# Units of steps 18 and 20 placed between the K tiles of the step's dense block, in a two-layer decoder trunk on one core

## The chip, the cores and the metric

The kernel runs on 1 core of one Trainium2 chip. The metric is device time in microseconds of one execution, and a profile of one execution goes with it. All times below are from the profile or the timed runs.

## The reference

The reference is one inference step of a decoder trunk of 2 layers, width 1024, on 256 prompt tokens and 8 single-token samples (264 columns together). In each layer the input is projected once, three groups of mixer heads work side by side on the parts, their outputs are projected together, and an MLP follows:

```python
proj = jnp.einsum('btd,de->bte', x, w_in)
hq, hf, hi, hg, rq, rk, rv, rg, su = jnp.split(proj, cuts, axis=-1)
...
o_hg, s_hg_new = _chunked_gated_linear(silu(hq), k_hg, hi, log_f, s_hg)     # 6 heads, gated
...
o_rt, s_rt_new = _chunked_gated_linear(q_r, k_r, rv, log_f_r, s_rt)         # 6 heads, retention
...
y5, s_re_new, s_im_new = _s5_scan(su, ...)
y5 = jax.nn.gelu(y5)
y5 = y5 * jax.nn.sigmoid(y5 @ s5_glu_w + s5_glu_b)
mixed = jnp.concatenate([o_hg, o_rt, y5], axis=-1).astype(x.dtype) @ w_out
x = _layer_norm(ALPHA * x + mixed, ln1_w, ln1_b)
ff = jnp.square(jax.nn.relu(x @ w_up)) @ w_down
x = _layer_norm(ALPHA * x + ff, ln2_w, ln2_b)
```

The outputs are the new activations and the new states of the three head groups, for prompt and samples.

## The kernel before

Every engine has a program of its own, written out by hand, and the programs meet on semaphores. The large matrices are cut into blocks of 128 output rows and 1024 inputs (512 KB). One block is one **step**. A layer has steps 0 to 22 for the input projection (one tile of 128 features each: the state-space input, the gated heads, the retention heads, and in steps 17 to 22 six tiles of output gates), 23 to 30 for the output projection, and the steps of the MLP behind them.

In a step TensorE (PE) runs the **dense** block: eight K tiles, each 128 inputs deep, which add up into one of three stream banks of PSUM (`dense`, L1051). A block is either read as it lies, one float32 matmul for each K tile (L1084, "unsplit"), or split into a high and a low part first, three matmuls for each K tile (L1109, L1110, L1111). ScalarE (ACT) makes the high part (`split_high`, L1165, its instruction L1172), VectorE (DVE) the low part (L1642). The split parts have three slots. `UNSPLIT` (L188) says which steps stay unsplit: in layer 0 steps 18 to 22 are split, in layer 1 steps 19 to 22. When the last matmul of a dense block is done, the semaphore `chunk_done` rises. ACT and DVE read the stream bank only behind that.

Beside the dense blocks stand the **units**: small pieces of matmul work of the mixers, each writing one of four mix banks in turn (`MIX_BANKS`). A unit waits until the unit four places ahead of it has been copied out of the bank. The table `PLAN` (L91 and the `_plan` calls) gives each step a list of units, and PE's loop runs them behind the step's dense block, unless `STOPS` (L172) has numbers for the step. Then the first units of the list stand between K tiles, each behind the number of K tiles that is given:

```python
stops = STOPS[l].get(c, ())
for at, to, u in zip((0,) + stops, stops, PLAN[l][c]):
    dense(l, c, range(at, to))
    units[u[0]](l, u)
...
    dense(l, c, range(stops[-1] if stops else 0, 8))
...
for u in PLAN[l][c][len(stops):]:
    units[u[0]](l, u)
```

The units that matter here are these. Step 18 of layer 0: two `glu` units (L943, four long matmuls in all), then transposes on PE (`transposes`, all at L734): `tr_hkd` twice, `tr_rv_sample`, `tr_rk_sample`, `tr_rv` twice, then two `ret_score` (L907, L910). Step 18 of layer 1 has the same without `glu` and `tr_hkd`. Step 20 of both layers: `ret_kv` twice (L857), `ret_o` three times (L932 to L936), `ret_state` (L921).

ACT and DVE run in the order of their own programs, step by step, too. At its step 19 in layer 0 ACT first splits block 21 (L1172), which takes the slot of block 18 and so waits for `chunk_done` of step 18, then does the gate sigmoid of step 18's tile (`gate_sigmoid`, L1222), then the sigmoid of the two `glu` banks (L1316), the copies of the two `tr_hkd` banks (L1326), of `tr_rv_sample` (L1349), of `tr_rk_sample` (L1352) and of `tr_rv` (L1356). In layer 1 the split of block 21 comes a step later there, because its load waits for the unsplit block 18. At its step 21 DVE first does the output gate of step 20's tile (`output_gate`, L1941, behind ACT's sigmoid of that tile), then adds the two `ret_kv` banks to the retention state and so empties them (`ret_sample_add`, L1966). `ret_k_decay` (L1983) on DVE empties the banks of two transposes of step 17.

The queue of SyncE (SP) loads the weight blocks in order into three raw slots, each behind the last reader of the block that lay there. GpSimd (POOL) prepares the masked inputs of `ret_kv`.

Of the kernel before, what the change touches and what calls it, by code (L numbers as in the profile page):

```python
# [43 lines left out]
UP_A = OUT0 + KT  # L44
# [49 lines left out]
def _plan(step, *names, layers=range(DEPTH)):  # L94
    for layer in layers:
        PLAN[layer][step] += names
# [72 lines left out]
for _l in range(DEPTH - 1):  # L169
    _plan(TABLES_AT, *[("s5_tab_in", _l + 1, _t) for _t in range(4)], layers=(_l,))  # L170
    _plan(N_CHUNKS - 1, ("s5_tab_near", _l + 1), layers=(_l,))
STOPS = ({19: (3, 6), 21: (4,), 22: (2, 5, 6, 7), UP_A + 1: (3, 5)}, {17: (3, 6), 21: (4,), 22: (2, 4, 6), UP_A + 1: (3, 5)})  # L172
UNITS_OF = {"s5_out": lambda u: [], 
            **{_n: lambda u: [u[:1]] if u[1] == 0 else [] for _n in ("hg_o_sample", "ret_o_sample")},
            **{_n + "_shift": lambda u: [u[:1]] if u[1] == 0 else [] for _n in ("ln1", "ln2")},
# [36 lines left out]
def build(nc, xT, weights, vectors, matrices, constants, level_masks, state_hg, state_rt, state_s5,  # L212
          y_out, hg_p_out, rt_p_out, s5_p_out, hg_s_out, rt_s_out, s5_s_out):
    with ExitStack() as ctx:
# [422 lines left out]
        def _(pe):  # L637
# [481 lines left out]
            for l in range(DEPTH):  # L1119
                for c in range(N_CHUNKS):  # L1120
# [10 lines left out]
                    if c == UP_A:  # L1131
# [6 lines left out]
                        continue  # L1138
                    stops = STOPS[l].get(c, ())
                    for at, to, u in zip((0,) + stops, stops, PLAN[l][c]):  # L1140
# [1342 lines left out]
```

How the kernel before makes its waits and increments, by code:

```python
        def wait_unit(eng, l, name):  # L470
            if name[0] == "hg_level":
                r, h = name[1:]
                eng.wait_ge(level_done[h], 7 * l + r + 1)
            elif name[0] == "hg_far":
                eng.wait_ge(far_done[name[1]], l + 1)
            elif name[0] == "ret_score":
                eng.wait_ge(score_done[name[1] % 2], 3 * l + name[1] // 2 + 1)
            else:
                eng.wait_ge(unit_done, UNITS_DONE[l, name])
# [7 lines left out]
        def need(eng, s, n):  # L488
            if n > 0:
                eng.wait_ge(s, n)
# [13 lines left out]
        def wait_raw(eng, n):  # L505
            eng.wait_ge(raw_loaded[RAW_SLOT[n]], 16 * RAW_TURN[n])
# [1 line left out]
        def wait_raw_read(eng, n):  # L509
            if SPLIT[n]:
                eng.wait_ge(low_ready, split_count(n))
            else:
                eng.wait_ge(chunk_done, n + 1)
# [1 line left out]
        def dense_tile(eng, l, c):  # L516
            eng.wait_ge(chunk_done, l * N_CHUNKS + c + 1)
            g = l * N_TILES + tile_index(c)
            return stream_bank[g % STREAM_BANKS][:, 0:T], tile_free[g % STREAM_BANKS]
# [4 lines left out]
        @block.sync  # L525
# [5 lines left out]
            for n in range(1, DEPTH * N_CHUNKS):  # L531
                if n in (1, 2):
                    sp.wait_ge(x_loaded[2 * n - 1], 16)
                if RAW_PREV[n] is not None:
# [3 lines left out]
                sp.wait_ge(y_ready, m + 2)  # L538
                sp.dma_start(y_out[:, m:m + 2, :], X[:, m:m + 2, :]).then_inc(outs["y"], 16)
            sp.wait_ge(outs["y"], 16 * KT // 2)
```

## Time and profile before

| | |
|---|---|
| median of 3 runs | 746.35 us (746.32 to 747.8) |
| the profiled execution, its own time | 746.15 us |
| its span, first to last instruction | 744.3 us, 17116 instructions |
| PE busy | 709.1 us (95%) |
| PE weight loads busy | 652.6 us (88%) |
| DVE busy | 539.3 us (72%) |
| ACT busy | 403.2 us (54%) |
| mean granted clock of PE | 0.982 of 2.4 GHz |

Times in the views count from the start of the span. Layer 0's steps 18 to 20 lie between 112 and 138 us, layer 1's between 482 and 501 us. A float32 matmul shows as two records, so a count of x8 at L943 is four matmuls. The busy time of a matmul includes its way through the array, so the pace of a run of matmuls is read from the starts, not from the durations.

### The profile page before, as it was taken

Reading aid. Unit: us, or ns where it says so; the run is one execution under the profiler, and the core shown is the slowest. Engines: PE = TensorE matmul, PEld = TensorE weight load, DVE = VectorE, ACT = ScalarE, POOL = GpSimd, SP = SyncE. Lnnn points to the kernel's source line nnn. Section 1 sums busy time; section 2 is a strip of 40 time slices with the busy share of each in tenths; the row PEclk is TensorE's granted clock in tenths of the full one; section 3 lists DMA queues with packets and bytes.
Section 4 is the critical chain, followed back from the end, with each engine's and each line's share of the span. In section 5 each row is a group of like instructions: output and inputs, shape, how many; then the busy total and the mean of one; then the engine's idle time right before and its main releaser. Section 6 shows DMA issues by size and latency. Waiting matters only on the chain.

```text
span 744.3 us, 17116 instructions
## 1 busy us (share of the span) xinstructions
PE 709.1 (95%) x7028; PEld 652.6 (88%) x7028; DVE 539.3 (72%) x970; ACT 403.2 (54%) x761; POOL 43.4 (6%) x62
## 2 busy tenths in 40 slices
PE   8899799999999999999979899999999999999994
PEld 6787668778999999999969797877999999999993
DVE  7999775468788988965685886556878776555474
ACT  4521055446788467764558233355568755677342
POOL 3000012100000000000040001020000000000001
PEclk9999899999999999999989999999999999999998
DMA  8733134535565656555624312342646656666631
GB/s 287 277 115 88 41 97 152 190 116 168 148 194 168 195 175 188 182 170 170 177 67 138 110 38 86 133 163 55 216 119 200 187 176 179 190 174 188 177 114 59
DMA packets 31085, 112.88 MB, mean 152 GB/s; under 512 B 3648, under 2 KB 3888, under 8 KB 30624
## 3 DMA queue, kind: packets, MB, share of 16 engines
q1 hardware_dynamic: 28224, 100.78, 44.3%
q0 software_dynamic: 2208, 9.93, 3.6%
q8 instruction: 56, 0.92, 0.5%
q10 hardware_dynamic: 576, 1.08, 0.4%
q14 instruction: 21, 0.17, 0.1%
HBM read 107.20 MB, written 4.18 MB: 150 GB/s over the span
## 4 chain that ended last, share of the span: by engine, by line
PE 78%; DVE 7%; ACT 3%; issue 2%; DVEq 0%; ACTq 0%
PE stream L1109 21%; PE stream L1110 20%; PE stream L1111 20%; PE stream L1084 6%; PE mix L812 1%; DVE w_low L1642 1%; PE mix L1007 1%; PE mix L845 1%; PE mix L885 1%; PE mix L734 1%; PE mix L857 0%; DVE scratch L1989 0%; PE mix L994 0%; DVE scratch L2237 0%; PE y_bank L715 0%
## 5 line engine op out<-in xcount | busy, mean ns | idle before, releaser
L1642 DVE TENSOR_TENSOR w_low<-w_raw,w_high 128x1024 fp32r<-128x1024 f32 x161 | 196.9, 1224 | 106.9 <-ACT w_high L1172 105.5
L1172 ACT ACTIVATE w_high<-w_raw 128x1024 fp32r<-128x1024 f32 x161 | 170.4, 1058 | 152.2 <-PE stream L1111 138.9
L1109 PE MATMUL stream<-a_high,w_high 128*128 128x264 f32 x520 | 154.9, 298 | 5.3 <-DVE a_low L2251 5.3
L1110 PE MATMUL stream<-a_low,w_high 128*128 128x264 f32 x520 | 148.7, 286 | 0.0
L1111 PE MATMUL stream<-a_high,w_low 128*128 128x264 f32 x520 | 148.4, 285 | 0.0
L1109 PE MATMUL stream<-h_high,w_high 128*128 128x264 f32 x512 | 146.3, 286 | 0.0
L1111 PE MATMUL stream<-h_high,w_low 128*128 128x264 f32 x512 | 145.1, 283 | 0.0
L1110 PE MATMUL stream<-h_low,w_high 128*128 128x264 f32 x512 | 145.0, 283 | 0.0
L1109 PEld LDWEIGHTS stream<-a_high,w_high 128*128 128x128 f32 x520 | 99.1, 191 | 9.7 <-issue 8.0
L1110 PEld LDWEIGHTS stream<-a_low,w_high 128*128 128x128 f32 x520 | 99.5, 191 | 0.4
L1111 PEld LDWEIGHTS stream<-a_high,w_low 128*128 128x128 f32 x520 | 98.9, 190 | 0.0
L1084 PE MATMUL stream<-X,w_raw 128*128 128x264 f32 x400 | 95.5, 393 | 3.2 <-DMA w_raw<-in_weights 2.5
L1109 PEld LDWEIGHTS stream<-h_high,w_high 128*128 128x128 f32 x512 | 96.4, 188 | 0.5 <-DVE h_low L2222 0.4
L1110 PEld LDWEIGHTS stream<-h_low,w_high 128*128 128x128 f32 x512 | 96.5, 188 | 0.1
L1111 PEld LDWEIGHTS stream<-h_high,w_low 128*128 128x128 f32 x512 | 96.0, 188 | 0.0
L1084 PEld LDWEIGHTS stream<-X,w_raw 128*128 128x128 f32 x400 | 74.6, 191 | 21.0 <-issue 6.2
L1109 PE MATMUL stream<-pre_a,w_high 128*128 128x266 f32 x256 | 74.6, 291 | 0.0
L1111 PE MATMUL stream<-pre_a,w_low 128*128 128x266 f32 x256 | 72.9, 285 | 0.0
L1110 PE MATMUL stream<-pre_x,w_high 128*128 128x266 f32 x192 | 54.8, 286 | 0.0
L1109 PEld LDWEIGHTS stream<-pre_a,w_high 128*128 128x128 f32 x256 | 48.3, 189 | 2.7 <-issue 2.6
L1111 PEld LDWEIGHTS stream<-pre_a,w_low 128*128 128x128 f32 x256 | 48.2, 188 | 0.0
L1110 PEld LDWEIGHTS stream<-pre_x,w_high 128*128 128x128 f32 x192 | 36.4, 189 | 0.1
(393 smaller groups left out, 983.1 us busy)
## 6 DMA issues: line engine op xcount, KB each, us to landing
w_raw<-in_weights SPq DMA_DIRECT2D x189, 512.0 KB, 3.6
mats<-in_matrices POOLq DMA_DIRECT2D x2, 1024.0 KB, 6.6
S_hg<-in_state_hg POOLq DMA_DIRECT2D x2, 768.0 KB, 7.4
out_hg_s<-S_hg POOLq DMA_DIRECT2D x2, 768.0 KB, 4.1
consts<-in_constants POOLq DMA_DIRECT2D x1, 1499.5 KB, 8.5
X<-in_xT ACTq DMA_DIRECT2D x4, 264.0 KB, 5.0
out_y<-X SPq DMA_DIRECT2D x4, 264.0 KB, 2.1
S_rt<-in_state_rt POOLq DMA_DIRECT2D x2, 512.0 KB, 8.5
```

The source lines that it names most:

```text
L734: mm = pe.transpose(b[0:rows, 128 * i:128 * i + 128], src[:, i, cols], ident)
L812: mm = pe.matmul(banks[h][to:to + n, n * (2 * f + t):n * (2 * f + t) + n], kd[rows, f, left], qd[rows, f, right], start=True, stop=True, t ...
L845: mm = pe.matmul(b[64 * h:64 * h + 64, :].rearrange("p (b v) -> p b v", b=8), ks_tok[:, 128 * ft + 64 * h:128 * ft + 64 * h + 64], v_own[V ...
L885: mm = pe.matmul(b[:, at:at + 2], qs_hg[:, ft, 2 * bp:2 * bp + 2, :].rearrange("p b v -> p (b v)"), cv("pair_sum")[:, 0:2], start=True, st ...
L1007: mm = pe.matmul(b[at:at + BLOCK, 0:T], cv("model_mean")[:, 0:BLOCK], src[:, k, :], start=(k < first + 4), stop=(k >= KT - 4), tile_positi ...
L1084: mm = pe.matmul(bnk[:, 0:T], w_raw[:, RAW_SLOT[n], 128 * k:128 * k + 128], x[:, k, :], start=(kk == 0), stop=(kk == 7))
L1109: pe.matmul(bnk[:, 0:width], wh, xh, start=(first and kk == 0), stop=False)
L1110: pe.matmul(bnk[:, 0:width], wh, xl, start=False, stop=False)
L1111: mm = pe.matmul(bnk[:, 0:width], wl, xh, start=False, stop=(last and kk == 7))
L1172: act.activation(w_high[:, SPLIT_SLOT[n], :], w_raw[:, RAW_SLOT[n], :], ACT.Copy).then_inc(high_ready, 1)
L1642: put(tt(w_low[:, SPLIT_SLOT[n], :], w_raw[:, RAW_SLOT[n], :], w_high[:, SPLIT_SLOT[n], :].bitcast(F32), ALU.subtract), low_ready)
```

## The change

The change adds entries for steps 18 and 20 to `STOPS` in both layers. In step 18 of layer 0 the first four units stand behind 2, 4, 6 and 7 K tiles, elsewhere the first three behind 2, 4 and 6. No instruction that computes is added or taken away, and the programs of ACT, DVE, POOL and SP stay as they are.

```diff
-STOPS = ({19: (3, 6), 21: (4,), 22: (2, 5, 6, 7), UP_A + 1: (3, 5)}, {17: (3, 6), 21: (4,), 22: (2, 4, 6), UP_A + 1: (3, 5)})
+STOPS = ({18: (2, 4, 6, 7), 20: (2, 4, 6), 19: (3, 6), 21: (4,), 22: (2, 5, 6, 7), UP_A + 1: (3, 5)}, {17: (3, 6), 18: (2, 4, 6), 20: (2, 4, 6), 21: (4,), 22: (2, 4, 6), UP_A + 1: (3, 5)})
```

**PE, layer 0, the end of step 18.** Here `stream0` is the dense block's bank and `mix0` to `mix3` are the mix banks. Before, from the last dense matmul on (the two `glu`, the two `tr_hkd`, the sample transposes, the two `tr_rv`, the scores):

```order
L1111 MATMUL stream0<-a_high,w_low 128x264
L943 MATMUL mix3<-MIX,mats 128x264 x2
L943 MATMUL mix0<-MIX,mats 128x264 x2
L734 MATMUL mix1<-consts,scratch 128x128 x3
L734 MATMUL mix2<-consts,scratch 128x128 x3
L734 MATMUL mix3<-consts,MIX 8x128 x3
L734 MATMUL mix0<-consts,KR 8x128 x2
L734 MATMUL mix1<-consts,MIX 128x128 x3
L734 MATMUL mix2<-consts,MIX 128x128 x3
L907 MATMUL mix3<-QR,KR 128x256
L907 MATMUL mix0<-QR,KR 128x256
```

With the change, from the first `tr_hkd` on:

```order
L734 MATMUL mix1<-consts,scratch 128x128 x3
L1109 MATMUL stream0<-a_high,w_high 128x264
L1110 MATMUL stream0<-a_low,w_high 128x264
L1111 MATMUL stream0<-a_high,w_low 128x264
L734 MATMUL mix2<-consts,scratch 128x128 x3
L1109 MATMUL stream0<-a_high,w_high 128x264
L1110 MATMUL stream0<-a_low,w_high 128x264
L1111 MATMUL stream0<-a_high,w_low 128x264
L734 MATMUL mix3<-consts,MIX 8x128 x3
L734 MATMUL mix0<-consts,KR 8x128 x2
L734 MATMUL mix1<-consts,MIX 128x128 x3
L734 MATMUL mix2<-consts,MIX 128x128 x3
```

Four units have moved ahead of the last K tile (the two `glu` stand behind two and four K tiles, above this piece), and the units behind the dense block begin with the one that writes `mix3` again, the bank of the first `glu`.

**ACT, layer 0, its step 19**, the same before and with the change; in brackets the semaphores that each instruction waits for:

```order
L1172 ACTIVATE w_high<-w_raw 128x1024 [waits chunk_done,raw_loaded0]
L1222 ACTIVATE late<-stream0 128x264 [waits chunk_done]
L1316 ACTIVATE X1<-mix3,vecs 128x264 [waits unit_done]
L1316 ACTIVATE X1<-mix0,vecs 128x264 [waits gel_ready,unit_done]
L1326 ACTIVATE scratch<-mix1 128x384 [waits gel_ready,unit_done]
L1326 ACTIVATE scratch<-mix2 128x384 [waits kt_ready,unit_done]
L1349 ACTIVATE late<-mix3 8x384 [waits kt_ready,unit_done]
L1352 ACTIVATE late<-mix0 8x256 [waits vs_ready,unit_done]
```

Nothing has moved here: the copies out of the mix banks stand behind two instructions that wait for a dense block.

**PE, layer 0, the end of step 20.** Before, behind the dense block (`ret_kv` twice, `ret_o` three times, `ret_state`):

```order
L857 MATMUL mix2<-late 32x512 x4
L857 MATMUL mix3<-scratch,late 32x512 x2
L932 MATMUL mix0<-scratch,V_tok 64x128 x2
L934 MATMUL mix0<-scratch,V_tok 64x128 x2
L936 MATMUL mix0<-scratch,V_tok 64x128 x2
L932 MATMUL mix1<-scratch,V_tok 64x128 x2
L934 MATMUL mix1<-scratch,V_tok 64x128 x2
L936 MATMUL mix1<-scratch,V_tok 64x128 x2
L932 MATMUL mix2<-scratch,V_tok 64x128 x2
L934 MATMUL mix2<-scratch,V_tok 64x128 x2
L936 MATMUL mix2<-scratch,V_tok 64x128 x2
L921 MATMUL mix3<-V_tok,scratch 32x64 x12
```

With the change, from the last K tile on:

```order
L1109 MATMUL stream2<-a_high,w_high 128x264
L1110 MATMUL stream2<-a_low,w_high 128x264
L1111 MATMUL stream2<-a_high,w_low 128x264
L932 MATMUL mix1<-scratch,V_tok 64x128 x2
L934 MATMUL mix1<-scratch,V_tok 64x128 x2
L936 MATMUL mix1<-scratch,V_tok 64x128 x2
L932 MATMUL mix2<-scratch,V_tok 64x128 x2
L934 MATMUL mix2<-scratch,V_tok 64x128 x2
L936 MATMUL mix2<-scratch,V_tok 64x128 x2
L921 MATMUL mix3<-V_tok,scratch 32x64 x12
```

Both `ret_kv` and the first `ret_o` have moved ahead of the last K tiles. The third `ret_o` and `ret_state`, which write the banks of the two `ret_kv` again, stay behind the dense block.

## Rows read from the trace of the kernel before

**Rows 1.** The page's chain that ended last, shares of the span.

```profile
PE 78%; DVE 7%; ACT 3%; issue 2%; DVEq 0%; ACTq 0%
```

**Rows 2.** Timeline of PE, step 18 of layer 0: start, length, instruction [idle before].

```profile
112.49 0.39 PE L1109 MATMUL stream<-a_high,w_high 128*128 128x264 f32 x1
112.71 0.29 PE L1110 MATMUL stream<-a_low,w_high 128*128 128x264 f32 x1
...
115.50 1.94 PE L943 MATMUL mix<-MIX,mats 128*128 128x264 f32 x8
117.28 0.82 PE L734 MATMUL mix<-consts,scratch 128*128 128x128 f32 x6
117.94 0.49 PE L734 MATMUL mix<-consts,MIX 128*8 128x128 f32 x3
...
120.61 0.70 PE L907 MATMUL mix<-QR,KR 32*128 32x256 f32 x4 [0.65 <-ACTq L1163]
...
121.47 0.39 PE L1109 MATMUL stream<-a_high,w_high 128*128 128x264 f32 x1
```

**Rows 3.** Timeline of ACT, the same stretch.

```profile
115.77 1.06 ACT L1172 ACTIVATE w_high<-w_raw 128x1024 fp32r<-128x1024 f32 x1 [2.90 <-PE stream L1111]
...
120.05 0.37 ACT L1352 ACTIVATE late<-mix 8x256 f32<-8x256 f32 x1
```

**Rows 4.** Timeline of DVE, the same stretch.

```profile
113.05 0.99 DVE L1983 TENSOR_TENSOR scratch<-mix,consts 128x256 f32<-128x256 f32 x2
```

**Rows 5.** Timeline of PE, step 20 of layer 0.

```profile
132.85 0.28 PE L1111 MATMUL stream<-a_high,w_low 128*128 128x264 f32 x1
...
133.95 1.02 PE L857 MATMUL mix<-scratch,late 8*32 8x512 f32 x4
134.90 0.44 PE L932 MATMUL mix<-scratch,V_tok 128*64 128x128 f32 x4
...
137.59 0.39 PE L1109 MATMUL stream<-a_high,w_high 128*128 128x264 f32 x1
```

**Rows 6.** Timeline of ACT and DVE, step 20 of layer 0.

```profile
133.18 0.39 ACT L1222 ACTIVATE late<-stream 128x264 f32<-128x264 f32 x1 [1.72 <-PE stream L1111]
...
134.24 1.63 DVE L1966 SCALAR_TENSOR_TENSOR S_rt<-S_rt,consts,mix 128x512 f32<-128x512 f32 x2
```

**Rows 7.** Timeline of ACT and PE, step 18 of layer 1.

```profile
486.64 0.39 ACT L1222 ACTIVATE late<-stream 128x264 f32<-128x264 f32 x1 [1.43 <-PE stream L1084]
...
488.14 0.70 PE L907 MATMUL mix<-QR,KR 32*128 32x256 f32 x4 [0.33 <-ACTq L1163]
```

**Rows 8.** Timeline of PE and DVE, step 20 of layer 1.

```profile
495.56 0.28 PE L1111 MATMUL stream<-a_high,w_low 128*128 128x264 f32 x1
...
498.05 1.63 DVE L1966 SCALAR_TENSOR_TENSOR S_rt<-S_rt,consts,mix 128x512 f32<-128x512 f32 x2
...
499.89 0.64 PE L921 MATMUL mix<-V_tok,scratch 128*32 128x64 f32 x24
...
500.46 0.39 PE L1109 MATMUL stream<-a_high,w_high 128*128 128x264 f32 x1
```

**Rows 9.** Stretches: length, busy time (records) of each engine, PE clock, DMA.

```profile
88.00:90.00 2.00, 0.00 (x0) 0.00 (x0) 0.00 (x0) 0.00 (x0) 0.00 (x0) 1.00 0.42 162
148.00:150.00 2.00, 1.13 (x10) 0.44 (x8) 1.68 (x4) 1.36 (x4) 0.00 (x0) 1.00 0.34 47
151.00:151.25 0.25, 0.25 (x3) 0.20 (x2) 0.20 (x1) 0.25 (x1) 0.00 (x0) 0.80 0.50 197
152.00:154.00 2.00, 2.00 (x9) 0.84 (x9) 1.58 (x3) 0.48 (x1) 0.00 (x0) 0.50 0.00 0
154.50:154.75 0.25, 0.25 (x2) 0.22 (x2) 0.25 (x1) 0.25 (x2) 0.00 (x0) 0.87 0.00 0
```

**Rows 10.** Timeline of PE, the same matmuls of step 23 and 24 in both layers.

```profile
153.25 4.01 PE L1084 MATMUL stream<-MIX,w_raw 128*128 128x264 f32 x14
...
512.24 3.38 PE L1084 MATMUL stream<-MIX,w_raw 128*128 128x264 f32 x14
```

## The prediction

> **What bounds the kernel now.** I read the chain that ended last first [rows 1]: 78% of the span lies on PE, 2% on issue and nothing on a DMA, so what delays PE in a stage delays the end unless a later wait takes it back. Then PE's timeline of step 18 in layer 0 [rows 2]: eight K tiles from 112.49 to 115.50, then the step's units, then step 19 at 121.47. The reader should see that this tail lasts 5.97 us and that PE waits in it, 0.65 us at the last pair of scores, for ACT. ACT's timeline says why [rows 3]: ACT idles 2.90 us until "PE stream L1111", the last dense matmul, and only then starts a row of work: the split of weight block 21 (its slot was step 18's, so it waits for that step's dense block), the gate sigmoid of step 18's tile, and behind them, in ACT's order, the copies that empty the four mix banks, down to L1352 at 120.05 (0.37 long). PE's L907 follows 0.19 later. So the tail is not a PE chain. It is an ACT chain of 121.47 - 115.50 = 5.97 us that begins where the dense block ends.
>
> **Step 18, layer 0.** The two glu units and two of the transposed units now stand in front of the last K tile, so the dense block ends later by what they take. Glu: 117.28 - 115.50 = 1.78 us for two. Transposes: 117.94 - 117.28 = 0.66 for six, 0.11 each [rows 2]. A dense run that starts behind a short unit is slow once: 112.71 - 112.49 = 0.22 to the second matmul, against (115.50 - 112.71)/23 = 0.12 for the other steps; 0.10 more, twice here (behind the long glu matmuls I take nothing): 0.20. One new wait: the first glu would stand at 112.49 + 0.22 + 5 x 0.12 = 113.31, and its bank is freed by DVE's first L1983 [rows 4], 113.05 + about 0.42 + about 0.19 until PE moves (estimates: a pair of 0.99 us with a gap in it, and the gap seen behind L1352) = 113.66: 0.35. Sum 1.78 + 0.66 + 0.20 + 0.35 = 3.0 us. ACT starts its chain 3.0 us later, and the chain is as long as before, since none of its copies waited for the units that move; the units left behind find their banks 3.0 later. PE, with less to do, idles some 2 us behind the dense block, and step 19 starts late by **3.0**. Bounds: 2.4 (units alone) and 3.3 (0.10 behind each glu too, and a little).
>
> **Step 20, layer 0.** Moved ahead of the last K tiles: both ret_kv and the first ret_o. Prices [rows 5]: the first ret_kv with the gap ahead of it 133.95 - (132.85 + 0.12) = 0.98, the second 134.90 - 133.95 = 0.95; the three ret_o and the state take 137.59 - 134.90 = 2.69, of which the state is 0.57 (500.46 - 499.89 in rows 8), so 0.71 for one ret_o. With three run starts of 0.10 the dense block ends 0.98 + 0.95 + 0.71 + 0.30 = 2.94 later. What hangs on that end [rows 6]: the gate sigmoid of step 20's tile, released by PE L1111; behind it DVE's output gate; behind that, in DVE's order, the two L1966 that empty the two ret_kv banks, the very banks that the third ret_o and the state need. L1966 starts 134.24 - 132.97 = 1.27 after the dense end. From there to the next step is 500.46 - 498.05 = 2.41 in layer 1, where the state did wait for the second L1966: 498.05 + 1.63 = 499.68, state at 499.89 [rows 8]. So the new tail is 1.27 + 2.41 = 3.68 us, however little PE has left. Before, it was 137.59 - 132.97 = 4.62, PE work that covered this chain; that cover goes. Net 2.94 + 3.68 - 4.62 = **2.0**; 1.6 with no run starts and no gap.
>
> **Step 18, layer 1.** Three transposed units, eight transposes at 0.11, move ahead: 0.88, and about 0.1 for run starts in all (the K tiles are single long matmuls here). ACT's gate sigmoid is released by PE L1084 and the copies of the first two banks stand behind it; PE already waits 0.33 for them at the scores [rows 7]. Net **1.0**, bounds 0.9 and 1.2. Weight block 21 is loaded when this dense block is done, so SP's queue moves by 1.0 too; the block is due at 500.46 [rows 8], over ten us on, and that costs nothing. POOL's blocks for ret_kv get their inputs later by the same shift, with as long to go.
>
> **Step 20, layer 1.** Same prices, 2.94, same tail, 3.68; before it was 500.46 - (495.56 + 0.12) = 4.78 [rows 8]. Net 2.94 + 3.68 - 4.78 = **1.8**; 1.4 at the least.
>
> Sum: 3.0 + 2.0 + 1.0 + 1.8 = **+7.8 us**, bounds 6.3 and 8.6. No PE wait further on takes it back: what PE waits for at the end of the mixer is DVE and ACT work that itself starts from PE units. The profiled execution took 746.15, 0.20 below the median of 746.35, so I add to the median: 754.2.
>
> **The clock.** PE's clock falls where its work thins out [rows 9]: in 148 to 150 PE worked 1.13 of 2 us, at 151.0 to 151.25 the granted clock is 0.80 on its way down, 152 to 154 lies at 0.50 (1.2 GHz), at 154.50 to 154.75 it is 0.87 on its way up: some 3.3 us at half rate, 1.65 us if PE has work throughout. A pair of rows agrees [rows 10]: fourteen L1084 records took 4.01 in layer 0, of which 154.5 - 153.25 = 1.25 us lay at the low clock, and 3.38 in layer 1: 0.63, half of 1.25. Not every gap does it: 88 to 90 stood still at full clock. The new tail of step 18 in layer 0 has 2.1 us of PE work in 6.0 (eleven transposes 1.21, scores 121.47 - 120.61 = 0.86), a longer thin stretch than 148 to 150, so I take one fall there: +1.65. By the Trainium skill, TensorE: Matmul & The Clock Gate, Part 1, the throttled clock is the default and activity lifts it; by that rule a tail this thin falls back to it and the time is 755.8, and without it 754.2. The trace agrees at 151 and not at 88. The other tails are shorter (3.7 us, half of it work); I take no fall there.
>
> 754.2 + 1.65 = **755.8 us**.
>
> **The rivals.** The waits as worked out, but no fall: 754.2, at the least 752.6. More falls, in the tails of step 20 too: 757.5, or 759.1 with two more.
>
> **Faster:** units between K tiles give ACT and DVE time to empty the banks, and PE's waits in the tails go. In layer 0's step 18 they are 5.97 less PE's work (1.78 + 0.66 + 1.21 + 0.86 = 4.51), 1.46; in layer 1's 0.33 [rows 7]; less run starts of 0.2 + 0.3 + 0.1 + 0.3 = 0.9: a gain of 0.9, 745.4. It decides from the point where ACT can empty a bank before the dense block has ended. Against it stands rows 3: ACT's first instruction there is released by the last dense matmul, and the copies stand behind it. The Trainium skill, Perfetto Trace Analysis, Matmuls, says that independent groups should rotate through different PSUM banks so that the evacuation of one overlaps the next group's matmuls; by that rule this change gains and the time is 745.4. The trace disagrees here: the banks rotate, but the evacuations stand behind a wait for the very block that they should overlap.
>
> **No change:** a later wait absorbs the delays, 746.4. For it speak PE's waits at the mixer's end; against it that they begin from PE's own units. That the change does not do what it says is excluded by the order of the built program.
>
> **How the numbers follow.** One fall 0.50, and its number is my time; no fall 0.22; more falls 0.18; faster 0.04; no change 0.04; 0.02 for a slowdown that I have not seen. The range 752.6 to 758.6 takes in the first two with their bounds and the nearer part of the third. Slower by over 0.2% (1.5 us, about what a measurement of this kernel can tell from no change) 0.92, within it 0.04, faster 0.04.
>
> **What would show it.** In the profile after, the dense block of step 18 in layer 0 takes 6.0 us from its first to its last matmul instead of 3.0, ACT's L1172 is still released by its end, and PE waits about 2 us for ACT at L734 behind it; in step 20 PE waits for DVE at L932 and L921, about 1.5 us together, in both layers; the clock lies at 0.50 for some 3 us in step 19 of layer 0. I am wrong if ACT's copies start before the dense end, if PE's new waits there stay under 1 us, or if step 21 of layer 0 starts 4 us late or more and the delay is gone by the up-projection.

## The result: slower by 15 us, where 9 were forecast

| | before | after |
|---|---|---|
| median | 746.34 us (745.1 to 747.8, 4 runs) | 761.73 us (761.39 to 764.23, 4 runs) |
| ratio to before, 95% interval | | 1.020 (1.017 to 1.023) |
| the profiled execution, and its span | 746.15 us, 744.3 us | 764.23 us, 762.3 us |
| mean granted clock of PE | 0.982 | 0.970 |

The direction was right and the size wrong: +15.4 us, and 761.7 lies above the range of 752.6 to 758.6. In the batches below the kernel before ran from 745.2 us (mean granted clock 0.983) to 752.4 us (0.973) from one execution to the next, so a part of a kernel is read from profiled executions stage by stage, and whole times only through ratios.

**Where it went.** Start of a step's first dense matmul in PE's timeline, less the same start in the profile of before (us; L0 is layer 0; each column is one of the kernels told of below):

| start of | before | after | a_18_l0 | b_20 | i_l1 | d_no19 | k_glu | e_act | f_act_dve | h_20_dve | j_best |
|---|---|---|---|---|---|---|---|---|---|---|---|
| L0 step 18 | 112.49 | 1.84 | -0.58 | -0.87 | 1.12 | 0.01 | -0.25 | -0.48 | 1.05 | -0.53 | 0.76 |
| L0 step 19 | 121.47 | 5.24 | 2.75 | -0.92 | 1.08 | 3.58 | 2.61 | -1.01 | 0.52 | -0.57 | 0.22 |
| L0 step 20 | 129.96 | 12.55 | 10.06 | -0.92 | 1.07 | 7.49 | 2.62 | -1.02 | 0.51 | -0.58 | 0.22 |
| L0 step 21 | 137.59 | 14.98 | 10.11 | 3.00 | 1.07 | 9.90 | 2.61 | 1.40 | 1.39 | 0.29 | 0.22 |
| L0 step 25 | 161.30 | 13.40 | 10.11 | 3.00 | 1.12 | 9.89 | 1.02 | -0.19 | 1.39 | -1.29 | -1.38 |
| L1 step 18 | 482.77 | 14.89 | 13.38 | 3.10 | 3.54 | 10.01 | 3.03 | 0.03 | 4.48 | 2.63 | 0.46 |
| L1 step 19 | 488.99 | 15.70 | 13.37 | 3.09 | 4.35 | 10.83 | 3.03 | -0.37 | 4.08 | 2.62 | 0.06 |
| L1 step 20 | 492.66 | 15.69 | 13.37 | 3.08 | 4.35 | 10.84 | 3.03 | -0.37 | 4.09 | 2.62 | 0.06 |
| L1 step 21 | 500.46 | 17.95 | 13.36 | 5.33 | 6.61 | 13.09 | 3.03 | 1.89 | 4.81 | 3.33 | 0.53 |

A difference between two lines of a column is what a stage added. In the changed kernel: step 18 of layer 0 3.40 (forecast 3.0), **step 19 7.31** (forecast 1.65, the clock), step 20 2.43 (2.0), step 18 of layer 1 0.81 (1.0), step 20 of layer 1 2.26 (1.8). The 1.84 ahead of step 18 is no part of the change: the program is the same up to there. It is most of the 2.5 us by which this profiled execution lies above the median.

PE's timeline of the changed kernel, step 18 of layer 0 and the starts of steps 19 and 20, answers to [rows 2] (start, length, instruction, idle before and its releaser):

```profile
114.32 0.39 PE L1109 MATMUL stream<-a_high,w_high 128*128 128x264 f32 x1
...
120.10 0.28 PE L1111 MATMUL stream<-a_high,w_low 128*128 128x264 f32 x1
122.39 0.49 PE L734 MATMUL mix<-consts,MIX 128*8 128x128 f32 x3 [2.00 <-ACTq L1163]
...
125.29 1.06 PE L907 MATMUL mix<-QR,KR 32*128 32x256 f32 x4 [0.63 <-ACTq L1163]
...
126.71 0.59 PE L1109 MATMUL stream<-a_high,w_high 128*128 128x264 f32 x1
127.09 0.42 PE L1110 MATMUL stream<-a_low,w_high 128*128 128x264 f32 x1
127.31 0.42 PE L1111 MATMUL stream<-a_high,w_low 128*128 128x264 f32 x1
...
142.51 0.40 PE L1109 MATMUL stream<-a_high,w_high 128*128 128x264 f32 x1
```

A dense block ends where its last L1111 starts, plus the 0.12 us from one of its matmuls to the next: here 120.10 + 0.12 = 120.22. The dense block now takes 120.22 - 114.32 = 5.90 us (6.0 was forecast), and PE then idles 2.00 us for ACT. In step 19 the matmuls start 0.22 apart where they started 0.12 apart in [rows 2]. ACT's timeline of the changed kernel, against [rows 3]:

```profile
120.49 1.06 ACT L1172 ACTIVATE w_high<-w_raw 128x1024 fp32r<-128x1024 f32 x1 [5.89 <-PE stream L1111]
...
124.73 0.37 ACT L1352 ACTIVATE late<-mix 8x256 f32<-8x256 f32 x1
```

ACT's chain still starts behind the last dense matmul and is as long as it was: L1352 ends 120.05 + 0.37 - 115.50 = 4.92 us after the dense end in [rows 2, 3], and 124.73 + 0.37 - 120.22 = 4.88 here. PE's waits in the changed kernel (us in total, times, longest), against 0.65 and 0.33 at L907 [rows 2, 7] and none at L932:

```profile
PE mix L932 <- DVEq L1621: 2.5, 2, 1.2
PE mix L734 <- ACTq L1163: 2.2, 2, 2.0
...
PE mix L907 <- ACTq L1163: 1.8, 2, 1.1
```

PE's timeline, step 20 of layer 0, against [rows 5]:

```profile
143.24 0.28 PE L1111 MATMUL stream<-a_high,w_low 128*128 128x264 f32 x1
143.45 1.06 PE L857 MATMUL mix<-late 8*32 8x512 f32 x8
144.44 0.39 PE L1109 MATMUL stream<-a_high,w_high 128*128 128x264 f32 x1
...
148.79 0.28 PE L1111 MATMUL stream<-a_high,w_low 128*128 128x264 f32 x1
...
151.12 0.44 PE L932 MATMUL mix<-scratch,V_tok 128*64 128x128 f32 x4 [1.24 <-DVEq L1621]
...
152.57 0.39 PE L1109 MATMUL stream<-a_high,w_high 128*128 128x264 f32 x1
```

And the stretches of the changed kernel (length, PE busy and records, granted clock, DMA share, GB/s), against [rows 9]:

```profile
120.00:122.00 2.00, 0.39 (x4) 1.00 0.73 219
122.00:124.00 2.00, 1.37 (x8) 1.00 0.29 70
124.00:126.00 2.00, 1.31 (x8) 0.88 0.65 236
126.00:128.00 2.00, 2.00 (x12) 0.50 0.03 8
...
140.00:142.00 2.00, 2.00 (x32) 0.50 0.48 182
142.00:144.00 2.00, 2.00 (x26) 0.86 0.00 0
...
162.00:164.00 2.00, 1.14 (x8) 1.00 0.53 213
```

PE works 3.07 of 6 us from 120 to 126; then the clock lies at 0.50 from 126 to 142, with PE's records filling every stretch. With the 0.48 us at half rate in 124 to 126 (0.12 x 2 / 0.5) and 0.56 in 142 to 144, that is some 17 us at 1.2 GHz. The fall of [rows 9] at 151 is gone: its place, now 162 to 164, shows 1.00, and 1.58 come back between steps 21 and 25.

### The profile page after: what moved, and what is told of

Read it like the earlier page. It is cut to its first block, busy times and chain, and to the rows that moved or that the text cites. A ratio compares the mean times of both kernels' runs of the same rounds, so it can differ in the third digit from the quotient of the medians.

```text
span 762.3 us, 17116 instructions
## 1 busy us (share of the span) xinstructions
PE 723.6 (95%) x7028; PEld 664.4 (87%) x7028; DVE 539.7 (71%) x970; ACT 403.2 (53%) x761; POOL 43.1 (6%) x62
## 3 DMA queue, kind: packets, MB, share of 16 engines
q10 hardware_dynamic: 576, 1.08, 0.4%
## 4 chain that ended last, share of the span: by engine, by line
PE 78%; DVE 7%; ACT 3%; issue 2%; DVEq 0%; ACTq 0%
PE stream L1109 21%; PE stream L1110 20%; PE stream L1111 20%; PE stream L1084 6%; PE mix L812 1%; DVE w_low L1642 1%; PE mix L885 1%; PE mix L734 1%; PE mix L1007 1%; PE mix L845 1%; PE mix L943 1%; PE mix L857 1%; DVE scratch L1959 0%; DVE scratch L1989 0%; PE mix L994 0%
## 5 line engine op out<-in xcount | busy, mean ns | idle before, releaser
L1109 PE MATMUL stream<-a_high,w_high 128*128 128x264 f32 x520 | 157.8, 304 | 5.3 <-DVE a_low L2251 5.3
L1110 PE MATMUL stream<-a_low,w_high 128*128 128x264 f32 x520 | 150.3, 289 | 0.0
L1111 PE MATMUL stream<-a_high,w_low 128*128 128x264 f32 x520 | 150.0, 288 | 0.0
L1111 PE MATMUL stream<-h_high,w_low 128*128 128x264 f32 x512 | 145.1, 283 | 0.0
L1109 PEld LDWEIGHTS stream<-a_high,w_high 128*128 128x128 f32 x520 | 100.7, 194 | 13.6 <-issue 11.9
L1110 PEld LDWEIGHTS stream<-a_low,w_high 128*128 128x128 f32 x520 | 101.2, 195 | 0.5
L1111 PEld LDWEIGHTS stream<-a_high,w_low 128*128 128x128 f32 x520 | 100.6, 193 | 0.0
L1084 PE MATMUL stream<-X,w_raw 128*128 128x264 f32 x400 | 99.6, 405 | 0.9 <-DMA X<-in_xT 0.6
L1111 PEld LDWEIGHTS stream<-h_high,w_low 128*128 128x128 f32 x512 | 96.0, 188 | 0.0
L1084 PEld LDWEIGHTS stream<-X,w_raw 128*128 128x128 f32 x400 | 77.7, 199 | 18.8 <-issue 3.9
L1111 PE MATMUL stream<-pre_a,w_low 128*128 128x266 f32 x256 | 72.9, 285 | 0.0
L1111 PEld LDWEIGHTS stream<-pre_a,w_low 128*128 128x128 f32 x256 | 48.2, 188 | 0.0
```

The source lines that it names most:

```text
L1084: mm = pe.matmul(bnk[:, 0:T], w_raw[:, RAW_SLOT[n], 128 * k:128 * k + 128], x[:, k, :], start=(kk == 0), stop=(kk == 7))
L1109: pe.matmul(bnk[:, 0:width], wh, xh, start=(first and kk == 0), stop=False)
L1110: pe.matmul(bnk[:, 0:width], wh, xl, start=False, stop=False)
L1111: mm = pe.matmul(bnk[:, 0:width], wl, xh, start=False, stop=(last and kk == 7))
```

## The experiments

The theories: **T1**, in step 18 ACT's chain hangs on the end of the dense block, so what stands ahead of that end is paid in full; **T2**, in step 20 DVE's two L1966, which empty the `ret_kv` banks, hang on the end of the dense block in the same way, through the output gate ahead of them; **T3**, the tail of layer 0's step 18 is so thin that the clock falls behind it. Rivals: the cut-up dense block itself costs the time (run starts), or the clock would fall there in any case. Where an expectation calls a rival T2 or T3, it means the rival that it states there.

### Parts alone: a_18_l0, b_20, i_l1

`a_18_l0` has the new stops of step 18 in layer 0 alone, `b_20` those of step 20 in both layers, `i_l1` those of steps 18 and 20 in layer 1.

```diff
-STOPS = ({19: (3, 6),
+STOPS = ({18: (2, 4, 6, 7), 19: (3, 6),
```

> Step 18 of layer 0 alone has its units between K tiles. Theory T1 (the tail behind the dense block is an ACT chain, and the thin tail drops PE's clock): step 19 starts 3.4 us late as in the changed kernel, the clock falls at the end of that tail and stays at 0.50 for 10 us or more, costing 5 us or more; with the old fall at 151 us gone, some 754 us. Rival T2 (the clock's falls are a matter of chance, only the waits belong to the change): 3.4 us over the kernel before, 749.8 us.

```diff
-STOPS = ({19: (3, 6),
+STOPS = ({20: (2, 4, 6), 19: (3, 6),
...
-{17: (3, 6),
+{20: (2, 4, 6), 17: (3, 6),
```

> Step 20 of both layers alone has its units between K tiles. T1: the dense block ends 2.9 us later and the DVE chain behind it stays, +2.0 and +1.8 us, no new fall of the clock: 750.2 us, PE waiting for DVE at L932 and L921. Rival T3 (thin units between K tiles by themselves lower the clock): a low clock in or behind step 20 of either layer, 753 us or more.

```diff
-{17: (3, 6),
+{18: (2, 4, 6), 20: (2, 4, 6), 17: (3, 6),
```

> The change in layer 1 alone, layer 0 as before. Theory (the waits as in the changed kernel's profile): step 18 adds 0.8, step 20 adds 2.3, sum 3.1 us, 749.5 beside 746.4, and no fall of the clock beyond those of the kernel before. Rival (the changed kernel's losses in layer 1 come from layer 0's delay): under 1 us. Second rival (falls of the clock also come behind layer 1's tails): 5 us or more.

Measured: `a_18_l0` 759.56 us (757.09 to 762.32), ratio 1.0146 (1.0097 to 1.0196). Its step 18 adds 3.33 and its step 19 7.31, to the hundredth what the changed kernel's step 19 added. The time is above the 754 expected: the fall cost more than 5 us, and the fall of [rows 9] did not go (0.50 in 162 to 164). `b_20` 753.96 (750.13 to 757.66), 1.0074 (1.0043 to 1.0105): 2.25 in layer 1 and 3.92 in layer 0, where a short fall lay inside step 20 (0.86, 0.50 and 0.79 in the three stretches from 132 to 138, 3.4 us at half rate). Its first two stretches:

```profile
132.00:134.00 2.00, 2.00 (x10) 0.86 0.00 0
134.00:136.00 2.00, 2.00 (x15) 0.50 0.00 0
```

So the low clock in step 20 came that the rival of `b_20` names; the time, 0.74% or 5.5 us above the kernel before, lies between the theory's 3.8 and the rival's 6.6 or more. PE's records fill these stretches and the one ahead of them, so no thin tail explains this fall; what does stays open. `i_l1` 752.64 (748.29 to 754.65), 1.0047 (1.0023 to 1.0071), some 3.5 us: 0.81 for step 18 and 2.26 for step 20, the changed kernel's increments, without layer 0's delay. So the parts add up within their intervals, and most of the loss, 1.5% of 2.0%, comes from one of the four places, layer 0's step 18.

### PE's gap filled: c_fill

The changed kernel with 16 dense matmuls of no use behind the dense block of layer 0's step 18, and four more ahead of the second pair of scores; they write the bank that step 19 then starts afresh.

```diff
 for u in PLAN[l][c][len(stops):]:
+    if l == 0 and c == 18 and u[0] == "tr_rv_sample":
+        fill(16)
+    if l == 0 and c == 18 and u == ("ret_score", 4):
+        fill(4)
     units[u[0]](l, u)
```

> The changed kernel with 16 dense matmuls more behind the dense block of step 18 in layer 0 and 4 more ahead of its last scores; they write a bank that step 19 clears, into time in which PE waits. T1: the waits stay, the clock does not fall at the tail, and the 7 us that step 19 lost at half rate come back: 754 to 755 us. T2 and T3: PE's wait is filled to no use, 761.7 us or a little more.

PE's timeline of this kernel (the filler is L1121), and its stretches:

```profile
110.88 0.39 PE L1109 MATMUL stream<-a_high,w_high 128*128 128x264 f32 x1
...
116.76 2.10 PE L1121 MATMUL stream<-a_high,w_high 128*128 128x264 f32 x16
...
122.68 0.39 PE L1109 MATMUL stream<-a_high,w_high 128*128 128x264 f32 x1
...
131.19 0.39 PE L1109 MATMUL stream<-a_high,w_high 128*128 128x264 f32 x1
```

```profile
122.00:124.00 2.00, 2.00 (x19) 1.00 0.06 25
124.00:126.00 2.00, 2.00 (x20) 1.00 0.20 83
...
134.00:136.00 2.00, 2.00 (x9) 0.73 0.00 0
```

Step 18 took 122.68 - 110.88 = 11.80 us, 2.82 more than before: twenty matmuls more cost nothing, because PE was waiting. Step 19 took 8.51 us instead of 8.49, at full clock. The time is 755.69 us (753.3 to 760.05), ratio 1.010 (1.0035 to 1.0165): 6.0 below the changed kernel, though PE does more. A fall of 3.4 us now lies inside step 20, between 134 and 140, as in `b_20`. This is T3 shown: with the gap filled, the long fall is not there. The mean clocks of the other executions fit: 0.981 to 0.985 in three of the four, against 0.969 to 0.976 in the changed kernel; the fourth, of 760.05 us, has 0.974. And 2.82 is T1's price at full clock.

### Step 19 left whole: d_no19

In the changed kernel step 19 of layer 0 is itself cut by units after three and six K tiles. Here it is not.

```diff
-STOPS = ({18: (2, 4, 6, 7), 20: (2, 4, 6), 19: (3, 6), 21: (4,),
+STOPS = ({18: (2, 4, 6, 7), 20: (2, 4, 6), 21: (4,),
```

> The changed kernel with the dense block of step 19 in layer 0 left whole (its three units stand behind it). T1 with the addition that a low clock lasts as long as PE's dense work is cut up by thin units: the fall is there, but full clock returns within or just behind step 19, about 4 us sooner than in the changed kernel: 758 to 760 us. Rival (the length of the low stretch does not depend on that): 761.7 us.

The stretches:

```profile
122.00:124.00 2.00, 1.31 (x8) 0.82 0.77 250
124.00:126.00 2.00, 2.00 (x12) 0.50 0.01 4
...
128.00:130.00 2.00, 2.00 (x11) 0.50 0.78 283
130.00:132.00 2.00, 2.00 (x20) 0.98 0.00 0
132.00:134.00 2.00, 2.00 (x24) 0.88 0.06 12
134.00:136.00 2.00, 2.00 (x24) 0.50 0.73 254
136.00:138.00 2.00, 2.00 (x34) 0.77 0.03 4
```

The fall comes at the same place but ends at 130, when step 19's unbroken dense block has run; a second one of 3.4 us follows in its units. Step 19 adds 3.91 instead of 7.31. The time, 760.25 us (759.56 to 763.82), ratio 1.0164 (1.0116 to 1.0212), is just above the 758 to 760 expected and can't be told from the changed kernel's: the intervals overlap, and so do the mean clocks, 0.971 to 0.978 here and 0.969 to 0.976 there. Part of the 3.40 that step 19 saves goes again behind it, because here the fall of [rows 9] is there once more (0.50 in 162 to 164), where the changed kernel's profile got 1.58 back. That the length of a fall hangs on what PE has to do behind it is what these two profiled executions suggest; it is not shown. Nor do these runs separate what in the cut step might hold the clock back (the short matmuls of L885, the run starts).

### Two glu units only: k_glu

Layer 0's step 18 with the two `glu` units between K tiles and the transposes behind the block.

```diff
-STOPS = ({19: (3, 6),
+STOPS = ({18: (2, 4), 19: (3, 6),
```

> Layer 0's step 18 alone, and of it only the two glu units between K tiles, behind 2 and 4 of them; the transposes stay behind the dense block. Theory (ACT's chain hangs on the dense end): the dense block ends 1.8 us (the glu units) plus 0.4 (the wait of the first one for DVE and a gap) later, so step 19 starts 2.2 us late, PE waits some 1.6 us at the transposes or scores behind the dense block; of the clock I don't know whether this tail, with 0.7 us more PE work than the whole change leaves, still brings the long fall: with it 7 us more (about 755.5), without it 748.5. Rival (only the transposes' move costs, since they are what the copies wait for): step 19 starts less than 0.5 us late, 746.4.

PE's timeline and the stretches:

```profile
120.32 0.49 PE L734 MATMUL mix<-consts,MIX 128*8 128x128 f32 x3 [1.34 <-ACTq L1163]
...
124.08 0.39 PE L1109 MATMUL stream<-a_high,w_high 128*128 128x264 f32 x1
```

```profile
112.00:114.00 2.00, 2.00 (x11) 0.50 0.54 207
114.00:116.00 2.00, 2.00 (x11) 0.83 0.03 8
...
122.00:124.00 2.00, 1.32 (x11) 1.00 0.58 227
124.00:126.00 2.00, 2.00 (x20) 1.00 0.00 0
```

The last dense matmul ended at 118.15, so the tail lasts 124.08 - 118.15 = 5.93 us, as in [rows 2], with PE waiting in it: T1 again. Step 18 adds 2.86; some 1.2 of that is a fall that here began ahead of the step, at 111, and ended at 114.7 (an estimate: half of the 2.4 us of step 18 at half rate). Behind the tail the clock stayed at 1.00. The twelve timed executions, 754.8 us in the median, ratio 1.0081 (1.0047 to 1.0115), run from 749.0 to 760.1, eleven us apart, and the profiled one is at the low end, 749.35. The clock makes this spread: the mean granted clock goes from 0.983 in the shortest execution to 0.967 in the longest, and 0.016 of 750 us is 12 us of full clock (an estimate). Where the clock lay low in the longest of them no trace shows; that they have the long fall fits, and isn't shown.

### The order on ACT and DVE changed: e_act, f_act_dve, and the control g_before_act_dve

`e_act` is the changed kernel, and ACT at its step 19 copies step 18's mix banks before it splits block 21 and before the gate sigmoid.

```diff
     if split_late(n + 1):
         split_high(n + 1)
+    if c == 19:
+        copies_19(l)
     if split_ahead(n + AHEAD):
         split_high(n + AHEAD)
```

> The changed kernel, but ACT at its step 19 empties the banks of step 18's units before it splits block 21 and before the gate sigmoid, in both layers. T1 (order on ACT behind the dense end): PE's waits at L734 and L907 in step 18 go in both layers, no fall of the clock in step 19 of layer 0; what is left is step 20's 4 us: 749.5 to 751 us. Rival (the banks themselves, or the cut-up dense block, cost the time): 758 us or more.

ACT's and then PE's timeline of this kernel:

```profile
114.36 0.48 ACT L1229 ACTIVATE X<-mix,vecs 128x264 f32<-128x264 f32 x1 [1.99 <-PE mix L943]
...
120.81 1.06 ACT L1172 ACTIVATE w_high<-w_raw 128x1024 fp32r<-128x1024 f32 x1 [0.18 <-ACT V_tok L1243]
```

```profile
117.91 0.49 PE L734 MATMUL mix<-consts,MIX 128*8 128x128 f32 x3
...
120.45 0.39 PE L1109 MATMUL stream<-a_high,w_high 128*128 128x264 f32 x1
```

ACT empties the first bank at 114.36, inside the dense block, and the tail shrinks from 5.97 us [rows 2] to 120.45 - 117.91 = 2.54. Step 18 now gains, 0.53 in layer 0 and 0.40 in layer 1, and in the profiled execution (748.16 us) no fall follows. 750.87 us (747.72 to 757.59), ratio 1.0044 (1.0004 to 1.0083): ten us of the loss gone, with the interleaving still in place. That is T1, and it excludes that the cut-up dense block costs the time by itself. Five of the ten executions run from 752.4 to 757.6 us with mean clocks of 0.972 to 0.980, against 0.983 to 0.985 in the other five, so falls still come in some; no trace shows where.

`f_act_dve` adds the same on DVE: at its step 21 the two L1966 stand ahead of the output gate.

```diff
-if HGT < c <= HGT + 5:
-    output_gate(l, c - 1 - HGT)
 if c == 21:
     for i in range(2):
         ret_sample_add(l, i)
+if HGT < c <= HGT + 5:
+    output_gate(l, c - 1 - HGT)
+if c == 21:
     ret_sample_q(l)
```

> As the one with ACT's order changed, and DVE at its step 21 also empties the two ret_kv banks before the output gate of step 20's tile. T1: PE's waits at L932 and L921 go too; all of the loss is gone and the waits of the kernel before at the scores with it: 745 to 747 us. Rival: the loss of step 20 stays, 749.5 us or more.

750.3 us (748.18 to 752.84), ratio 1.0006 (0.9986 to 1.0026). By the ratio the loss is gone, as expected; the 745 to 747 us are missed because the kernel before itself ran at 749.55 in this batch. Step 20 adds 0.87 and 0.72 instead of 2.43 and 2.26: T2's wait is worth some 1.5 us in each layer. The control is the kernel before with both reorders:

> The kernel before with both orders changed and the units behind the dense blocks, as a control. If the orders alone carry the gain: the 0.65 and 0.33 us waits at the scores go, 745.3 to 746 us, as fast as the one with units between K tiles. If the place of the units matters too, that one is faster by 0.5 us or more.

747.46 us (746.03 to 751.57), ratio 0.9982 (0.9959 to 1.0005); its stages move by -0.16 and -0.01 (step 18) and 0.00 and -0.17 (step 20). So the reorders alone give next to nothing, and with them interleaving gains 0.4 in each step 18, and loses 0.9 in each step 20. In whole times the kernel with units between K tiles is not the faster one.

### Step 20 without its wait: h_20_dve

The stops of step 20 alone, with DVE's order changed as above.

> Step 20 of both layers alone with its units between K tiles, and DVE's order changed. T1: no wait of PE on DVE in step 20, within 1 us of the kernel before: 745.5 to 747 us. Rival T3: 749 us or more.

749.74 us (744.98 to 751.93), ratio 0.9988 (0.9962 to 1.0013). DVE's timeline:

```profile
131.44 0.75 DVE L1966 SCALAR_TENSOR_TENSOR S_rt<-S_rt,consts,mix 128x512 f32<-128x512 f32 x1 [2.77 <-PE mix L857]
...
136.38 0.49 DVE L1941 SCALAR_TENSOR_TENSOR late<-late,vecs,stream 128x264 f32<-128x264 f32 x1 [2.32 <-ACT late L1222]
```

By the ratio no loss can be told; the 745.5 to 747 us expected are missed for the same reason as above. The first bank is emptied five us before the gate, no PE wait for DVE at L932 is left, and yet the step adds 0.87 in layer 0 and 0.71 in layer 1: that is what three cuts cost by themselves, 0.2 to 0.3 each.

### A version built on the finding: j_best

Steps 18 interleaved, steps 20 as before, ACT's copies ahead.

```diff
-STOPS = ({19: (3, 6),
+STOPS = ({18: (2, 4, 6, 7), 19: (3, 6),
...
-{17: (3, 6),
+{18: (2, 4, 6), 17: (3, 6),
...
+    if c == 19:
+        copies_19(l)
```

> Steps 18 of both layers interleaved as in the change, step 20 left behind its dense block, and ACT's copies of step 18's banks put ahead of the split of block 21 and of the gate sigmoid. Theory (the loss in step 18 is the copies' place behind the wait for the dense block): the stage of step 18 gains 0.5 in layer 0 and 0.4 in layer 1, no fall of the clock behind it, all in all 0.9 us faster than before, 745.5 beside 746.4. Rival (interleaving costs gaps whatever ACT does, and the gains seen with the reordered ACT are the reorder's alone): 0.0 to 0.5 slower than before. Second rival (the clock falls there anyway): 5 us or more slower.

747.45 us (744.69 to 751.15) beside 748.17 of the kernel before in the same batch, ratio 0.9991 (0.997 to 1.0012): no difference that can be told. The steps 18 gained 0.54 and 0.40 as expected, and layer 1's step 20, which is untouched, lost 0.47. ACT's timeline there:

```profile
491.50 1.06 ACT L1172 ACTIVATE w_high<-w_raw 128x1024 fp32r<-128x1024 f32 x1 [2.19 <-DMA w_raw<-in_weights]
...
497.52 0.39 ACT L1222 ACTIVATE late<-stream 128x264 f32<-128x264 f32 x1
```

Before, this split began at 490.29: block 21 is loaded only when the unsplit dense block of step 18 is done, which interleaving makes later. The gate sigmoid behind it came at 497.52 instead of 496.99, DVE's L1966 with it, and PE waited 0.33 us at L932.

## Why the prediction was wrong, point by point

- **What bounds the kernel** held: chains on ACT and DVE that begin at a dense block's end. The chain that ended last has the same shares as [rows 1].
- **Step 18, layer 0**, 3.0: held. At full clock it is 2.82 in c_fill; the 3.40 of the changed kernel has 0.56 of the clock in it, since the scores from L907 to step 19 took 126.71 - 125.29 = 1.42 us instead of the 0.86 of [rows 2].
- **Step 18, layer 1**, 1.0: 0.81, just under the bound of 0.9. The later load of block 21 cost nothing, as forecast: step 20 adds 2.26 with it (i_l1) and 2.25 without (b_20). In j_best, where step 20 is whole, it costs 0.47.
- **Step 20**, 2.0 and 1.8: measured 2.43 and 2.26. The tail was right, 152.57 - 148.91 = 3.66 against 3.68. The dense block became 6.40 us long, 3.39 more where 2.94 was taken: a ret_kv with its gaps cost 144.44 - 143.36 = 1.08, not 0.98 or 0.95, and a ret_o 0.90, not 0.71. A unit's price had been taken from units that stood in a row, without the gap to the dense run on either side.
- Waits together: 2.8 + 2.4 + 0.8 + 2.3 = 8.3 us, against 7.8 and bounds of 6.3 and 8.6 (the upper bounds that the prediction works out add up to 8.3). This half of the sum held.
- **The clock** is the step that failed: "so I take one fall there: +1.65". The place and the cause were right (a_18_l0, c_fill), the size was not: 7.31 in step 19 and 0.56 in the scores, 7.9 us. The price was copied from the fall at 151 [rows 9], behind which PE ran long unsplit matmuls and was back at full clock after 3.3 us. Behind step 18 stands a step cut up by units of short matmuls (L885), and there the clock stayed down for 17 us, in the changed kernel and in a_18_l0 alike. The range's upper end counted more falls of 3.3 us, never a longer one. By the Trainium skill, TensorE: Matmul & The Clock Gate, Part 1, the throttled clock is the default state and activity releases it. The fall behind the thin tail agrees with that; the 16 us at 0.50 behind it, in which PE's records fill every stretch, do not, and neither does the fall in `b_20`.
  Longer falls stood in the trace of the kernel before, as these stretches in the form of [rows 9] show: 0.51, 0.50, 0.50 and 0.78, which is 6.8 us at half rate. Another 6.8 us lie at 380 to 387, and PE stood still for part of both. The price was taken from a shorter one. Even so 17 us is far more, and why the clock stayed down so long is open.

```profile
76.00:78.00 2.00, 1.23 (x64) 0.93 (x53) 1.93 (x4) 0.00 (x0) 0.00 (x0) 0.51 0.04 8
...
80.00:82.00 2.00, 2.00 (x56) 1.73 (x48) 1.93 (x5) 0.00 (x0) 0.00 (x0) 0.50 0.04 8
82.00:84.00 2.00, 2.00 (x9) 1.63 (x8) 1.56 (x7) 0.00 (x0) 0.00 (x0) 0.78 0.00 0
```

- Left over, between 16.2 (8.3 + 7.9) and the 18.0 by which the two spans differ: -1.6 for the vanished fall at 151, +1.5 between the layers, where a fall that lasted 3.4 us at 424 lasted 6.8 at 436, and +1.84 ahead of the change.
- **The faster rival** (banks rotate, so evacuations overlap): not in this kernel, for the reason given. With ACT's order changed it comes true, as e_act shows, though for 0.5 us and not 0.9. The rule drawn on there, in the Trainium skill, Perfetto Trace Analysis, Matmuls, holds here once the evacuating engine is free to run: with ACT's copies ahead, the tail is 2.54 us instead of 5.97.

## What to carry to other kernels

Before moving units in front of a dense block's end, look at what the evacuating engines have queued ahead of the copies: if that waits for the same block, each moved unit delays the whole chain, and PE's own saving turns into idle time. Move the copies first; here that took back ten us of a loss of fifteen. Even then interleaving gained nothing that whole times can tell (j_best, 0.9991): by stages it won 0.9 us and lost 0.5 to a weight load that came later. When a new thin stretch is made on PE, price the clock by the longest fall in the trace and not by the nearest, look at what PE runs behind it, and give the range room for a fall several times as long.

## What the runs showed of the hardware

- A fall of the clock can last far longer than the thin stretch at which it begins: 17 us at 1.2 GHz behind 6 us in which PE worked 3.07, 6.8 us behind the same tail when the step after it ran unbroken (d_no19), none when twenty matmuls filled the tail (c_fill); each is the profiled execution of its kernel.
- The same gap does not always bring a fall. The stretch of [rows 9] at 88 stood still at full clock; in the changed kernel's profiled execution, with the same program up to there, the clock fell just behind that place (0.84, 0.50 and 0.80 in 90 to 92, 92 to 94 and 94 to 96), which is most of the 1.84 us. And the thin stretch of [rows 9] at 148, with 1.13 us of PE work in 2, has a fall behind it in the kernel before and none in the changed kernel, where it shows 1.14 at 162.
- Useless matmuls in a wait can pay: twenty of them made the changed kernel 6 us faster (c_fill, still 1.0% slower than the kernel before).
